# A diagonal of factors in place of the unit matrix in the turning product of an attention

## What is computed

```python
def masked_softmax(s, mask):
    s = jnp.where(mask, s, NEG_INF)
    m = jnp.max(s, axis=-1, keepdims=True)
    e = jnp.where(mask, jnp.exp(s - m), 0.0)
    z = jnp.sum(e, axis=-1, keepdims=True)
    return e / jnp.where(z > 0, z, 1.0)

o_cmp, p_cmp = compressed_branch(q_a, kc, vc, slopes_nsa)
o_slc = selected_branch(q_a, kv_a[2], kv_a[3], idx, valid, slopes_nsa)
o_win = banded_attention(q_a, kv_a[4], kv_a[5], slopes_nsa, NSA_WINDOW, None)
g = jax.nn.sigmoid(g_nsa).reshape(B, S, NSA_KV_HEADS, NSA_GROUP, 3)
o_a = (g[..., 0:1] * o_cmp + g[..., 1:2] * o_slc + g[..., 2:3] * o_win)
o_b = banded_attention(q_b, k_b, v_b, slopes_swa, SWA_WINDOW, sinks[l])
```

## Time and profile before

| | us |
|---|---|
| median of 3 runs | 3193.94 |
| their range | 3193.71 to 3194.86 |
| the profiled execution, own time | 3193.26 |
| its span, first to last instruction | 3191.1 |

### The profile page before, as it was taken

How to read it: one execution, slowest core, us unless ns; L and a number is a source line. 1 busy time by engine, 2 the same in 40 slices (tenths; PEclk the granted TensorE clock), 3 DMA queues, 4 the chain that set the end, 5 groups by cost and what they waited for, 6 DMA issues and landing times.

```text
span 3191.1 us, 32848 instructions
## 1 busy us (share of the span) xinstructions
PE 3020.4 (95%) x13352; PEld 2200.5 (69%) x13352; DVE 1420.8 (45%) x3127; ACT 472.8 (15%) x1040; POOL 314.8 (10%) x303
## 2 busy tenths in 40 slices
PE   9999999979999999999999799999999988997985
PEld 7886444946888866888864448888855566885321
DVE  7563311434555334554346826554333056663113
ACT  1101010001001021001022221001021075012101
POOL 0000100111000100000111230000100084001110
PEclk9999999689999999999999899999999999998998
DMA  5222222102222212222212012222212300227996
GB/s 206 80 82 84 86 79 81 39 27 73 93 93 80 94 65 106 93 79 93 93 54 79 30 40 99 79 93 93 93 66 106 119 28 22 85 93 298 425 425 282
DMA packets 54348, 345.46 MB, mean 108 GB/s; under 512 B 7984, under 2 KB 8112, under 8 KB 15536
## 3 DMA queue, kind: packets, MB, share of 16 engines
q1 hardware_dynamic: 44496, 319.84, 26.5%
q10 hardware_dynamic: 5088, 15.06, 1.2%
q0 software_dynamic: 4608, 8.40, 0.7%
HBM read 336.97 MB, written 14.68 MB: 110 GB/s over the span
## 4 chain that ended last, share of the span: by engine, by line
PE 87%; DVE 5%; DMA 4%; ACT 1%; issue 1%; SPq 1%; POOL 0%; ACTq 0%; DVEq 0%; POOLq 0%
PE bank L832 52%; PE bank L483 18%; PE bank L492 4%; PE bank L1466 2%; PE bank L2668 2%; DMA ring<-in_weights 2%; PE bank L519 1%; PE bank L513 1%; PE bank L1718 1%; PE bank L1702 1%; PE bank L1493 1%; DVE area L1763 1%; DMA buf_b<-in_weights 1%; PE bank L2685 1%; DMA norm<-in_weights 1%
## 5 line engine op out<-in xcount | busy, mean ns | idle before, releaser
L483 PE MATMUL bank<-area,ring 128*128 128x512 f32 (+1 forms) x964 | 335.1, 509 | 19.6 <-DVE area L1596 15.6
L832 PE MATMUL bank<-buf_b,mixed 128*128 128x256 f32 x1472 | 334.3, 379 | 0.0
L832 PE MATMUL bank<-area,mixed 128*128 128x256 f32 x1504 | 333.7, 379 | 0.0
L854 DVE TENSOR_TENSOR mixed<-ring 128x512 f32<-128x512 f32 (+2 forms) x144 | 96.0, 666 | 506.8 <-PE bank L832 500.1
L832 PE MATMUL bank<-buf_a,mixed 128*128 128x256 f32 x1408 | 319.8, 379 | 0.0
L832 PEld LDWEIGHTS bank<-area,mixed 128*128 128x128 f32 x1504 | 285.8, 190 | 38.9
L832 PEld LDWEIGHTS bank<-buf_b,mixed 128*128 128x128 f32 x1472 | 279.7, 190 | 38.0
L483 PEld LDWEIGHTS bank<-area,ring 128*128 128x128 f32 x964 | 163.4, 191 | 188.3 <-issue 169.3
L832 PEld LDWEIGHTS bank<-buf_a,mixed 128*128 128x128 f32 x1408 | 267.6, 190 | 36.8 <-DVE mixed L862 0.4
L832 PE MATMUL bank<-buf_b,ring 128*128 128x256 f32 x1184 | 271.5, 379 | 0.4 <-ACT buf_b L712 0.4
L832 PE MATMUL bank<-buf_a,ring 128*128 128x256 f32 x1056 | 244.1, 380 | 7.9 <-DMA buf_a<-in_x 7.5
(11 more groups left out here) (392 smaller groups left out, 3289.9 us busy)
## 6 DMA issues: line engine op xcount, KB each, us to landing
ring<-in_weights SPq DMA_DIRECT2D x241, 1024.0 KB, 4.8
area<-in_weights SPq DMA_DIRECT2D x27, 1024.0 KB, 29.1
buf_a<-in_weights SPq DMA_DIRECT2D x11, 1024.0 KB, 28.0
buf_b<-in_weights SPq DMA_DIRECT2D x10, 1024.0 KB, 28.5
mixed<-in_weights SPq DMA_DIRECT2D x6, 1024.0 KB, 28.2
norm<-in_weights SPq DMA_DIRECT2D x6, 1024.0 KB, 28.0
area<-chosen SPq DMA_DIRECT2D x8, 512.0 KB, 7.4
buf_a<-in_x ACTq DMA_DIRECT2D x4, 512.0 KB, 7.4
```

What stands on the lines that cost most here:

```text
L483: mm = pe.e.matmul(bank[0:w.shape[1], 0:n], w, x[k], start=k == 0, stop=k == len(pieces) - 1)
L832: mm = pe.e.matmul(b, w[:, k * P:(k + 1) * P], x(INPUT_OF[p], unit.lo + k), start=(unit.key, BANK_OF[p]) not in begun, stop=unit.last and ...
L854: made = tt(unit.mix("S1"), unit.quarter("A21"), unit.quarter("A22"), ALU.add)
```

## The change

The factor goes to where the chunk is turned. GpSimd no longer multiplies the exponentials: for each branch it multiplies the unit matrix, 128x128, by the branch's factors, one for each partition, into a tile of its own. TensorE turns a chunk of that branch with this diagonal in the unit matrix's place, which gives the turned chunk with its factors in it. That call is `matmul` and no longer `transpose`. There are 24 such tiles, three for each of eight items in turn, twelve in free memory of `area` and twelve in `norm`; GpSimd waits, before it writes those of an item, until the turns of the item eight before are done. Only `att_n` is given such tiles.

```diff
@@ class Attention, __init__ @@
-            self.on_dve, self.pools = on_dve, pools
+            self.on_dve, self.pools, self.factors = on_dve, pools, factors
+            for i, item in enumerate(items):
+                if factors:
+                    n = len(item["parts"])
+                    item["factors"] = [factors[i % (len(factors) // 3) * 3 + j] for j in range(n)]
@@ tensor @@
                         for c in range(lo, hi, P):
-                            mm = transpose(pe, b[:, c:c + P], item["slot"][k][:, c:c + P])
+                            if self.factors:
+                                j = sum(map(len, item["groups"][:k])) + sum(br["at"] + br["width"] <= c for br in group)
+                                mm = pe.e.matmul(b[:, c:c + P], item["slot"][k][:, c:c + P], item["factors"][j], start=True, stop=True)
+                            else:
+                                mm = transpose(pe, b[:, c:c + P], item["slot"][k][:, c:c + P])
@@ pool @@
                 po.wait_ge(self.z_ready, i // len(self.batches[0]) + 1)
+                if self.factors and i >= len(self.factors) // 3:
+                    before = i - len(self.factors) // 3
+                    po.wait_ge(*g.done((self.name, "t", before, len(self.items[before]["groups"]) - 1)))
                 for j, (l, _) in enumerate(item["parts"]):
-                    made = po.e.tensor_scalar(l, l, item["zs"][:, j:j + 1], None, ALU.mult)
+                    out, src = (item["factors"][j], C("ident")) if self.factors else (l, l)
+                    made = po.e.tensor_scalar(out, src, item["zs"][:, j:j + 1], None, ALU.mult)
@@ memory and att_n @@
-    n_turned = [sp_n.get(T) for _ in range(8)]
+    n_turned, n_factors = [sp_n.get(T) for _ in range(8)], [sp_n.get(P) for _ in range(12)] + [norm[:, i * P:(i + 1) * P] for i in range(12)]
-                      2, lambda i, n: i % 2 == 0 and n == 0, ((0, 1, 2, 3), (4, 5, 6), (7,)))
+                      2, lambda i, n: i % 2 == 0 and n == 0, ((0, 1, 2, 3), (4, 5, 6), (7,)), n_factors)
```

More of the change, by code:

```diff
@@ L1625, in build_in, with __init__ @@
     class Attention:
-        def __init__(self, name, items, rings, turned, stats, batch, on_dve, pools):
+        def __init__(self, name, items, rings, turned, stats, batch, on_dve, pools, factors=None):
             self.name, self.items, self.stats = name, items, stats
```

## The result

| | before | changed |
|---|---|---|
| median of 13 runs each, us | 3193.43 | 3201.92 |
| their range, us | 3191.82 to 3195.6 | 3199.04 to 3204.76 |
| profiled execution, own time, us | 3193.26 | 3199.5 |
| its span, us | 3191.1 | 3197.4 |

The ratio is 1.0027, with a 95% interval of 1.0019 to 1.0036: slower by 8.5 us, 6 to 11.5 by the interval. The forecast was slower by 14, in a range of 3200 to 3217.

A forecast was written before the change was run, and what follows sets the result against it. TensorE bounds the attention, paced by a loop with VectorE's reading of scores. Gated tiles +8.3, tile 3 +3.4, sliding heads +4.2 and clock -1.5 sum to +14.4 us, rounded to +14: median 3208, range 3200 to 3217.

The forecast's parts named there:

- Gated tiles: Second block's attention, query tiles 0 to 2: doubled turns, partly covered by waits for VectorE, add 2.75 us a tile, +8.3.
- its sign: In the attention, a warm gated tile should take 24.5 to 25 us instead of 22.2.
- Tile 3: Last gated tile, beside which sliding heads start: b=0 +0.23, b=1 +1.15, b=2 +1.61, b=3 +0.4 us; sum +3.4.
- followed at once by other TensorE work: Tile 3, turns of b=1 at 2635.55: no wait covers the doubling, so it costs the full +1.15 us.
- Sliding heads: Attention's sliding tiles, 56 chunks: +0.9 us a tile for 3.7 tiles and 0.9 for the drain, +4.2.
- The clock: Low-clock stretches in gated tiles: busier TensorE takes half of their cost back, -1.5 us; bounds -2.75 and +3.5.
- should arrive at the end undiminished: After the attention: TensorE runs without a break, so the attention's gain or loss reaches the total time in full.
- TensorE pays nearly everything: Rival, attention's turns: slack moves away instead of being used; +21 to +28 us, 3215 to 3222. Chance 0.12.
- the clock stays up: Rival, weak stretches of the attention: true products keep 2.4 GHz everywhere; +8 us or below, 3198 to 3202. Chance 0.12.
- VectorE's side alone decides: Rival, nothing measurable: 1.5 us a gated tile, 1.8 in the sliding part, clock back; +5, 3199. Chance 0.06.
- Products still one record: Rival, attention's turns: the change doesn't do what it says; about -1.5 us, 3192. Chance 0.02.
- Faster through GpSimd: Rival: GpSimd holds tile 3 (-4.6 us) and the sliding batches (-9.6); net -7, 3187. Chance 0.04.

The follow-up runs named there:

- the kernel with all stalls filled: The kernel before, with unused true products put into TensorE's stalls through the attention and ahead of the last norm's scales: 3188.64 us beside 3195.48; repeated, 3189.59 beside 3194.05.
- the first two kernels: Against the kernel before: true products with the unit matrix, GpSimd still multiplying in place, 3201.71 us; GpSimd's diagonals made but chunks turned in transpose mode, 3196.01; before, 3194.97.
- the two parts of the change: The change in gated tiles 0 to 3 only (184 of 240 chunks), 3206.27 us; in sliding tiles 4 to 7 only (56 chunks), 3200.51; kernel before beside them, 3193.37.

## Why the prediction was right, and where its sizes were off

The direction and the mechanism held: two records at the turns' pace, an attention bound by TensorE, GpSimd's relief without effect. The size did not: +14 against +8.5. The time lies 1.9 us inside the lower end of the range, an end that was put there for the rivals, so that the range held by little, and partly by luck. Step by step, from turns' start to the next turns' start. Warm values of before are from the earlier trace rows, b=0 from the kernel with all stalls filled (2605.55 to 2610.11), since the one of the earlier trace rows ends in a low stretch.

| | before | changed | more | forecast |
|---|---|---|---|---|
| from b=1 | 4.66 | 5.07 | 0.41 | 0.68 |
| from b=2 | 6.06 | 6.74 | 0.68 | 0.95 |
| from b=3 | 6.89 | 7.59 | 0.70 | 0.90 |
| from b=0 | 4.56 | 4.83 | 0.27 | 0.23 |
| gated tile | 22.17 | 24.23 | 2.06 | 2.75 |
| tile 3 from b=1 to the first sliding turns | 15.89 | 17.52 | 1.63 | 3.2 |
| sliding part | 33.46 | 37.29 | 3.83 | 4.2 |

**Gated tiles.** The size that was off comes from taking a row before for the bare work. Turns of 10, 14 and 16 chunks took 1.57, 1.92 and 2.03 us to the next scores, 0.13 to 0.16 a chunk and not 0.115, since they contain a hidden wait: the turns of a batch are four groups, their pool has three banks, and the fourth group waits until VectorE (L1743) has copied the first out. The loads of the unit matrix in the kernel before show it, behind 8 of 10 turns and behind 11 of 14:

```profile
2591.82 0.20 PEld L519 LDWEIGHTS bank<-const,area 128*128 128x128 f32 x2 [0.34 <-DVE area L1743]
...
2596.72 0.31 PEld L519 LDWEIGHTS bank<-const,area 128*128 128x128 f32 x3 [0.26 <-DVE area L1743]
```

With doubled records TensorE gets to the fourth group later and doesn't wait. The turns take 2.43, 3.32 and 3.77 us, which is 0.86, 1.40 and 1.74 more, and not 1.15, 1.61 and 1.84. That is 0.29, 0.21 and 0.10 less than I put in, nearly the whole miss of each row of the table. A turn's record took what I had said, (3.84-0.28)/31 = 0.115 us; the row it was set against held a wait.

The part that VectorE's reading covers I had nearly right, 0.47, 0.66 and 0.94 us. From the first record of the scores to the products with values it fell from 1.85 to 1.40 us for b=1, from 2.46 to 1.74 for b=2 and from 2.96 to 1.92 for b=3, by 0.45, 0.72 and 1.04. In the kernel before, for b=2:

```profile
2597.20 0.40 PE L1702 MATMUL bank<-area 64*128 64x31 f32 x2
...
2599.66 1.75 PE L1718 MATMUL bank<-area 128*64 128x128 f32 x28
```

A warm gated tile takes 24.23 us, below the 24.5 to 25 that the forecast named as its sign. Three tiles: +6.2 and not +8.3.

**Tile 3.** Here a step failed, not only its size: that b=1 "is followed at once by other TensorE work, the full +1.15". The timeline of the changed kernel:

```profile
2638.20 2.50 PE L1734 MATMUL bank<-area 128*128 128x128 f32 x20
2640.63 0.70 PE L1706 MATMUL bank<-area 64*128 64x256 f32 x4
2642.22 1.31 PE L1722 MATMUL bank<-area 128*64 128x128 f32 x20 [0.89 <-ACT area L1753]
2643.46 3.39 PE L1734 MATMUL bank<-norm,area 128*128 128x128 f32 x28
...
2649.20 3.84 PE L1734 MATMUL bank<-norm,area 128*128 128x128 f32 x32
...
2655.72 0.71 PE L1734 MATMUL bank<-area 128*128 128x128 f32 x4
```

From the turns at 2638.20 to the products with values at 2642.22 it is 4.02 us. Before it was 4.02 us as well, and in the kernel with all stalls filled 4.02 once more (2631.66 to 2635.68); before, from the turns at 2635.55:

```profile
2639.57 1.31 PE L1718 MATMUL bank<-area 128*64 128x128 f32 x20 [0.49 <-ACT area L1745]
2640.81 1.99 PE L519 MATMUL bank<-const,area 128*128 128x128 f32 x14
...
2651.44 0.44 PE L519 MATMUL bank<-const,area 128*128 128x128 f32 x2
```

The scores did follow at once, but the products behind them wait for ScalarE, whose copies (L1753) stand behind its exponentials (L1811). The chain of the changed kernel at this place:

```profile
2637.84 3.33 ACT area L1811 x12
2641.17 0.92 ACT area L1753 x3
2642.22 1.31 PE bank L1722 x20
```

The doubling was free there, +0 and not +1.15, and so was the low stretch beside it, which I had priced at 0.8 us. b=2 paid 5.74-4.34 = 1.40 (forecast 1.61). b=3 paid 6.52-6.29 = 0.23 (0.4), with GpSimd's wait gone in it.

**Sliding heads.** This held. The turns of b=0 at 2664.70 and 2674.16:

```profile
2664.70 0.71 PE L1734 MATMUL bank<-area 128*128 128x128 f32 x4
...
2666.80 0.44 PE L1722 MATMUL bank<-area 128*64 128x128 f32 x4 [0.96 <-ACT area L1753]
...
2674.16 0.71 PE L1734 MATMUL bank<-area 128*128 128x128 f32 x4
```

9.46 us a tile against 8.56, the forecast's +0.9. The waits for ScalarE's copy are down to one a tile.

**The clock, and what follows the attention.** With the terms above the doubling costs some 11.9 us (11.4 to 12.0 by the lengths); I had 15.9. That is 4.0 of the 5.9 us by which the sum was over. The other 1.9 lie here: I gave the clock -1.5, and 11.9 less 8.5 is 3.4. Inside the attention the steadier clock gave the 2.6 us that lie between 131.81 and 129.18 in the first trace, and about nothing in the second (143.27-131.81 = 11.5). Another 0.8 to 1.9 us came behind the attention, where the low clock is the same before and after and part of the gain is a shorter wait for a transfer. So the clock's sign was right in one trace and its size is not settled by these. That "what the attention gains or loses should arrive at the end undiminished" was wrong by those 0.8 to 1.9 us, and that outside the attention "TensorE runs without a break" was wrong too: it stands still for 12.45 us before 2923.37.

**The rivals.** That TensorE pays nearly everything (+21 to +28): no, 27.6 us of records cost 11.4 to 12.0. That the clock stays up (+5 to +8): the time came out beside its upper end, though more by the smaller price than by the clock, which did fall in the second trace. That VectorE's side alone decides (+5, 1.5 a gated tile): no, a gated tile paid 2.06. Products still one record: no, 480. Faster through GpSimd: refuted by the first two kernels. The Trainium skill, "TensorE: Matmul & The Clock Gate", Part 4, says that transposes don't count as busy in the same way for the clock gate. The kernel with all stalls filled, in its repetition, has full clock in an attention with 240 transposes; but they never stand alone for more than 2.1 us there, between true products, so no run here decides that rule. The Trainium skill, the same page, terms table, has transposes 4x faster for FP32. The traces disagree: 480 records against 240, each 0.11 to 0.12 us from the next, are 2x.

## What to carry to other kernels

A scaling folded into a fp32 transpose wasn't free here: the transpose became a true product with two records a chunk, and with TensorE as the bound, the relief of an engine that was in time anyway bought nothing. Price such a step from start to start against what gates the next work, since merged rows hide waits, and ask of every "followed at once" what the second instruction behind it waits for. Before trusting a difference of some microseconds, tally low stretches of the clock in both traces, also far behind the change and by place in the program, since those of the slower kernel lie later in time, and look at a second trace of each. Filling the stalls with unused products gained 4.5 to 6.8 us here, but only when done at all of them.

## What the runs showed of the hardware

In the attention of the kernel before, TensorE's granted clock fell to half four times for 3.4 us, although no wait ahead of these stretches was longer than a microsecond; ahead of the one at 2611.80 TensorE was busy 2.03 of 3.25 us. The same instructions of the old attention had some 14 us of low clock in two traces and some 24 in a third, so that the places belong in part to the execution or the chip. Of the kernels with fillers, the one filled in the attention alone had 3.4 us there, and 17.1 at the last norm against 10.2 before; those filled everywhere had none and 3.4 us in the attention, and 10.2 and 6.8 at the norm. So unused products of 0.22 to 0.27 us each, in stalls of 0.4 to 2 us, kept the attention at full speed or nearly, and didn't rid the norm of its low stretch. Whether the fillers in the attention caused the longer stretch 200 us behind it, and why the two parts of the change cost 20 us together where the whole costs 8.5, is open; no run takes it apart.
